# Two inner layer seams: the next layer's first chunk of matmuls taken one block of tokens at a time

## The reference

```python
# layers 0 and 1
h = rms_norm(x, pre_norm_w[i])
y = gated_deltanet_mixer(h, ...) if i == 0 else short_conv_mixer(h, ...)
x = x + rms_norm(y, post_norm_w[i])
# short_conv_mixer: u, b_gate, c_gate, z = split(h @ w_in, 4)
# layer 2
shift, scale, gate = split(c @ w_ada + b_ada, 3)
h = rmsnorm(x, pre_norm_g) * (1 + scale) + shift
proj = h @ w_in          # split in q, k, v, z_ret, u_val, u_gate, z_conv, g_a, g_b
```

## Time and profile before

| | |
|---|---|
| Median of 3 runs | 862.86 us (862.37 to 863.36) |
| Profiled execution: time, span of its rows | 862.82 us, 860.7 us |
| TensorE busy, DVE busy, ACT busy | 849.1 us (99%), 725.1 us (84%), 495.3 us (58%) |
| Mean granted TensorE clock | 0.999 |
| Seam 1, from the end of `gdn_out` to the second chunk of `sc_in` | 256.90 to 269.86 us |
| Seam 2, from the end of `sc_out` to the second chunk of `glu` | 487.20 to 501.31 us |

### The profile page before, as it was taken

How to read it: one execution, slowest core, us unless ns; L and a number is a source line. 1 busy time by engine, 2 the same in 40 slices (tenths; PEclk the granted TensorE clock), 3 DMA queues, 4 the chain that set the end, 5 groups by cost and what they waited for, 6 DMA issues and landing times.

```text
span 860.7 us, 14398 instructions
## 1 busy us (share of the span) xinstructions
PE 849.1 (99%) x5404; PEld 747.8 (87%) x5404; DVE 725.1 (84%) x1154; ACT 495.3 (58%) x726; POOL 47.7 (6%) x48
## 2 busy tenths in 40 slices
PE   9999999999999999999999999999999999999997
PEld 8999998798888888888888799999887798888885
DVE  7798999757858888989879788999998999957864
ACT  6878856566547555555546574433446674545743
POOL 0001001241100000000000000000001230001000
PEclk9999999999999999999999999999999999999999
DMA  8774684700783777777785554554454536564431
GB/s 270 248 255 133 195 277 147 191 3 4 276 292 94 239 252 255 254 255 252 250 306 196 195 172 150 194 193 165 166 181 137 176 107 199 193 231 159 163 131 49
DMA packets 129423, 163.63 MB, mean 190 GB/s; under 512 B 17203, under 2 KB 91867, under 8 KB 129243
## 3 DMA queue, kind: packets, MB, share of 16 engines
q1 hardware_dynamic: 129371, 162.92, 57.4%
HBM read 158.68 MB, written 4.23 MB: 189 GB/s over the span
## 4 chain that ended last, share of the span: by engine, by line
PE 85%; DVE 7%; DMA 3%; ACT 2%; issue 2%; SPq 0%; DVEq 0%; ACTq 0%
PE psum L583 12%; PE psum L570 12%; PE psum L584 11%; PE psum L590 11%; PE psum L551 7%; PE psum L558 7%; PE psum L552 7%; PE psum L575 6%; PE psum L843 3%; DMA w_raw<-in_sc_w_out_dram 2%; DVE w_lo L1543 1%; DVE Tq L1819 1%; DVE outer L1817 1%; PE psum L726 1%; PE psum L962 1%
## 5 line engine op out<-in xcount | busy, mean ns | idle before, releaser
L1040 ACT ACTIVATE w_hi<-w_raw 128x1024 fp32r<-128x1024 f32 x263 | 275.2, 1058 | 199.2 <-PE psum L590 98.2
L1543 DVE TENSOR_TENSOR w_lo<-w_raw,w_hi 128x1024 fp32r<-128x1024 f32 x264 | 316.3, 1223 | 69.6 <-ACT w_hi L1040 67.2
L551 PE MATMUL psum<-hT,w_hi 128*128 128x256 f32 x544 | 135.4, 287 | 0.0
L552 PE MATMUL psum<-hT,w_hi 128*128 128x256 f32 x544 | 133.4, 283 | 0.0
L570 PE MATMUL psum<-hT,w_hi 128*128 128x512 f32 x496 | 124.2, 392 | 0.0
L583 PE MATMUL psum<-w_hi,hT 128*128 128x512 f32 x288 | 116.6, 405 | 0.0
L584 PE MATMUL psum<-w_hi,hT 128*128 128x512 f32 x288 | 112.4, 390 | 0.0
L2062 DVE SCALAR_TENSOR_TENSOR cv<-aP,par,cv 128x256 f32<-128x256 f32 x240 | 106.9, 514 | 0.0
L551 PEld LDWEIGHTS psum<-hT,w_hi 128*128 128x128 f32 x544 | 104.3, 192 | 0.5 <-issue 0.2
L552 PEld LDWEIGHTS psum<-hT,w_hi 128*128 128x128 f32 x544 | 104.3, 192 | 0.4 <-issue 0.2
L570 PEld LDWEIGHTS psum<-hT,w_hi 128*128 128x128 f32 x496 | 89.2, 189 | 15.9
(11 more groups left out here) (313 smaller groups left out, 1059.5 us busy)
## 6 DMA issues: line engine op xcount, KB each, us to landing
w_raw<-in_w_in_dram SPq DMA_DIRECT2D x44, 1024.0 KB, 5.0
w_raw<-in_sc_w_in_dram SPq DMA_DIRECT2D x32, 1024.0 KB, 7.4
w_raw<-in_gdn_w_in_dram SPq DMA_DIRECT2D x23, 1024.0 KB, 6.9
ada<-in_w_ada_dram SPq DMA_DIRECT2D x24, 512.0 KB, 4.8
w_raw<-in_gdn_w_out_dram SPq DMA_DIRECT2D x8, 1024.0 KB, 5.2
w_raw<-in_sc_w_out_dram SPq DMA_DIRECT2D x8, 1024.0 KB, 7.5
w_raw<-in_w_ret_out_dram SPq DMA_DIRECT2D x8, 1024.0 KB, 5.1
w_raw<-in_w_conv_out_dram SPq DMA_DIRECT2D x4, 1024.0 KB, 5.1
```

The source lines that it names most:

```text
L551: pe.matmul(o[:, m, :], w_hi[s][:, k, mine], a_hi[:, ka, :], start=m == 0 and ka == 0, stop=False, skip_group_check=True)
L552: pe.matmul(o[:, m, :], w_hi[s][:, k, mine], a_lo[:, ka, :], start=False, stop=False, skip_group_check=True)
L1040: act.activation(w_hi[j % 2 * 2 + h][:, :, :], raw[slot][:, h * KH2:(h + 1) * KH2, :], ACT.Copy).then_inc(hi_ready, 1)
L1543: return dve.tensor_tensor(o, whole, hi.bitcast(F32), ALU.subtract)
```

## The change

In both inner seams the work is cut by blocks of 128 tokens.

- DVE's `y_norm` now makes `xn` of block 0 before `x_next` of block 1. What is left of block 1's norm moves to a new `block_norms` on ACT and DVE, which takes the place of `pre_norm` for `n` of 1 and 2. On ACT: four evictions of block 0, the squares and the root of block 1, four evictions of block 0, eight of block 1 (in seam 2 also two `hx` per block), a copy of block 0's sums, the split of the next chunk's first half, a copy of block 1's sums. Each eviction is 128x128.
- TensorE's `first_tokens` takes the place of `pre_norm` and `first_chunk`: it turns block 0 and computes, with the activations stationary and the weights moving, the first chunk for these 128 tokens in halves, with the turning of block 1 in the middle. The fillers are one and three, after the turning of block 0.
- The sums of the first chunk now lie as tokens by channels. ACT copies them to `tok`, and `turn_back` turns them with four transposes inside the next chunk, behind its first matmuls on `w_hi` (`midway`). The other chunks are as before.
- The first sums of `sc_in` have no separate part any more: ACT drops one `sc_part` copy, DVE's `sc_whole` becomes a `tensor_copy`, and the loops of ACT and DVE have their first step written out (`apart`).
- `fold_modulation` moves from behind `sc_out` to between the two token blocks of its last chunk.
- The `held` bounds in `chunks` are written differently; with the values used (0 and 1) they give the same order. The outer seam (`n == 0`) is only renamed.

```diff
+            def turn_block(n, t):
+
+                for k in range(KT):
+                    if k % KH2 == 0:
+                        pe.wait_ge(xn_ready, (NT * n + t) * 2 + k // KH2 + 1)
+                    mm = pe.transpose(block_of(t, k), xn[:, t, k * P:(k + 1) * P], ident)
+                    if k % KH2 == KH2 - 1:
+                        mm.then_inc(turned, 1)
+
+            def first_tokens(n, g, fill):
+
+                def high(t, h):
                     s = g % 2 * 2 + h
-                    if g == 0 and h == 0:
-                        pe.wait_ge(quarter_hi, 1)
-                    else:
-                        pe.wait_ge(hi_ready, 2 * g + h + 1)
+                    pe.wait_ge(hi_ready, 2 * g + h + 1)
                     for k in range(h * KH2, (h + 1) * KH2):
-                        if g == 0 and k == 2:
-                            pe.wait_ge(hi_ready, 1)
-                        pe.wait_ge(hhi_ready, KT * n + k + 1)
-                        for m in range(2):
-                            mine = slice(m * P, (m + 1) * P)
-                            pe.matmul(o_hi[:, m, :], w_hi[s][:, k % KH2, mine], hT_hi[:, k, :], start=k == 0 and (m == 0 or apart), stop=False,
-                                      skip_group_check=True)
+                        pe.wait_ge(hhi_ready, highs_by(n, t, k))
+                        pe.matmul(sums_of(t), hT_hi[:, k, tokens(t)], w_hi[s][:, k % KH2, :], start=k == 0, stop=False, skip_group_check=True)
                     pe.wait_ge(lo_ready, 2 * g + h + 1)
                     for k in range(h * KH2, (h + 1) * KH2):
-                        for m in range(2):
-                            mine = slice(m * P, (m + 1) * P)
-                            pe.matmul(o_hi[:, m, :], w_lo[s][:, k % KH2, mine], hT_hi[:, k, :], start=False, stop=False, skip_group_check=True)
+                        pe.matmul(sums_of(t), hT_hi[:, k, tokens(t)], w_lo[s][:, k % KH2, :], start=False, stop=False, skip_group_check=True)
+
+                def low(t, h):
+                    s = g % 2 * 2 + h
                     for k in range(h * KH2, (h + 1) * KH2):
                         if k % 2 == 0:
-                            pe.wait_ge(h_ready, KT // 2 * n + k // 2 + 1)
-                        for m in range(2):
-                            mine = slice(m * P, (m + 1) * P)
-                            mm = pe.matmul(o_lo[:, m, :], w_hi[s][:, k % KH2, mine], hT_lo[:, k, :], start=False, stop=k == KT - 1, skip_group_check=True)
-                    mm.then_inc(half_done, 1)
-
-            def chunk(i, g0, j, a_hi, a_lo):
+                            pe.wait_ge(h_ready, lows_by(n, t, k))
+                        mm = pe.matmul(sums_of(t), hT_lo[:, k, tokens(t)], w_hi[s][:, k % KH2, :], start=False, stop=k == KT - 1, skip_group_check=True)
+                    return mm
+
+                turn_block(n, 0)
+                keep_clock(fill[0])
+                high(0, 0)
+                keep_clock(fill[1])
+                low(0, 0)
+                high(0, 1)
+                turn_block(n, 1)
+                low(0, 1).then_inc(block_done, 1)
+                high(1, 0)
+                high(1, 1)
+                low(1, 0).then_inc(half_done, 1)
+                low(1, 1).then_inc(block_done, 1)
+
+            def turn_back(n, o):
+
+                for t in range(NT):
+                    pe.wait_ge(tok_copied, NT * (n - 1) + t + 1)
+                    for m in range(2):
+                        mm = pe.transpose(o[:, m, tokens(t)], tok[:, t, m * P:(m + 1) * P], ident)
+                mm.then_inc(half_done, 1)
+
+            def chunk(i, g0, j, a_hi, a_lo, midway=None):
 
                 o = bank(j)
                 pe.wait_ge(bank_free, i * 4 + (g0 + j + 1))
@@ -550,6 +616,8 @@
                             ka = h * KH2 + k
                             pe.matmul(o[:, m, :], w_hi[s][:, k, mine], a_hi[:, ka, :], start=m == 0 and ka == 0, stop=False, skip_group_check=True)
                             pe.matmul(o[:, m, :], w_hi[s][:, k, mine], a_lo[:, ka, :], start=False, stop=False, skip_group_check=True)
+                    if midway is not None and h == 0:
+                        midway()
                     pe.wait_ge(lo_ready, i * 8 + (2 * (g0 + j) + h + 1))
                     for m in range(2):
                         mine = slice(m * P, (m + 1) * P)
@@ -558,7 +626,7 @@
                             mm = pe.matmul(o[:, m, :], w_lo[s][:, k, mine], a_hi[:, ka, :], start=False, stop=ka == KT - 1, skip_group_check=True)
                     mm.then_inc(half_done, 1)
 
...
+                        elif ahead and j == 0 and midway is not None:
+                            continue
...
             wide_deep("gdn_out", yT_hi, yT_lo, (y_op_ready, 0), start=(ROUNDS - OUT_FROM) // 2)
 
             pe.wait_ge(bank_free, 4 + FIRST["gdn_out"] + 4)
-            pre_norm(1, (5, 0))
-            keep_clock(1)
-            phase("sc_in", hT_hi, hT_lo, first=(1, psum[:, 0:2, 0:SEQ], psum[:, 0:2, SEQ:2 * SEQ], True))
-            wide_deep("sc_out", yT_hi, yT_lo, (y_op_ready, KT))
-
-
-            pe.wait_ge(ada_used, MOD_PARTS)
-            pe.wait_ge(bank_free, 4 + FIRST["sc_out"] + 4)
-            for q in range(P // BS):
-                mm = pe.matmul(psum[q * BS:(q + 1) * BS, 0, 0:3 * KT], fold[:, :], mod_p[:, :, q], start=True, stop=True)
-            mm.then_inc(mod_done, 1)
-            pre_norm(2, (4, 0))
-            keep_clock(1)
+            first_tokens(1, FIRST["sc_in"], (1, 3))
+            pe.wait_ge(tok_copied, 1)
+            phase("sc_in", hT_hi, hT_lo, midway=lambda: turn_back(1, psum[:, 0:2, 0:SEQ]))
+
+            def fold_modulation():
+                pe.wait_ge(ada_used, MOD_PARTS)
+                pe.wait_ge(bank_free, 4 + FIRST["sc_out"] + 4)
+                for q in range(P // BS):
+                    mm = pe.matmul(psum[q * BS:(q + 1) * BS, 0, 0:3 * KT], fold[:, :], mod_p[:, :, q], start=True, stop=True)
+                mm.then_inc(mod_done, 1)
+            wide_deep("sc_out", yT_hi, yT_lo, (y_op_ready, KT), between=fold_modulation)
+            first_tokens(2, FIRST["glu"], (1, 3))
```

On ScalarE:

```diff
+            def block_norms(n, g, gain, shift=None):
+
+                def highs(t, ks):
+                    for k in ks:
+                        act.wait_ge(turned, turned_by(n, t, k))
+                        if shift is None:
+                            act.activation(hT_hi[:, k, tokens(t)], block_of(t, k), ACT.Copy, scale=gain(k)).then_inc(hhi_ready, 1)
+                        else:
+                            act.activation(hT_hi[:, k, tokens(t)], block_of(t, k), ACT.Identity, scale=gain(k), bias=shift(k)).then_inc(hhi_ready, 1)
+                    if shift is not None and ks[-1] == KT - 1:
+                        for k in (KT - 2, KT - 1):
+                            act.activation(hx[:, k, tokens(t)], block_of(t, k), ACT.Identity, scale=gain(k), bias=shift(k)).then_inc(hhi_ready, 1)
+
+                def copied(t):
+                    act.wait_ge(block_done, 3 * (n - 1) + 2 + t)
+                    act.activation(tok[:, t, :], sums_of(t), ACT.Copy).then_inc(tok_copied, 1)
+
+                if shift is not None:
+                    act.wait_ge(mod_ready, 1)
+                    act.wait_ge(gain2_ready, 1)
+                highs(0, range(KH2))
+                for q in range(2):
+                    x_square(n, 1, q)
+                x_root(n, 1)
+                highs(0, range(KH2, KT))
+                highs(1, range(KT))
+                copied(0)
+                split_hi(g, 0, 1, 0)
+                copied(1)
...
                             x_square(n + 1, 0, 1)
                             x_root(n + 1, 0)
-                            for q in range(2):
-                                x_square(n + 1, 1, q)
-                            x_root(n + 1, 1)
```

On VectorE:

```diff
+            def block_norms(n, g, gain, shift=None):
+
+                def lows(t, h):
+                    ks = range(h * KH2, (h + 1) * KH2)
+                    if shift is None:
+                        dve.wait_ge(hhi_ready, highs_by(n, t, ks[-1]))
+                        for k in ks:
+                            i = dve.scalar_tensor_tensor(out=hT_lo[:, k, tokens(t)], in0=block_of(t, k), scalar=gain(k),
+                                                         in1=hT_hi[:, k, tokens(t)].bitcast(F32), op0=ALU.mult, op1=ALU.subtract)
+                            if k % 2:
+                                i.then_inc(h_ready, 1)
+                        return
+                    dve.wait_ge(hhi_ready, highs_by(n, t, ks[-1]) + 2 * h)
+                    for k in ks[:KH2 - 2 * h]:
+                        i = dve.tensor_scalar(hx[:, k, tokens(t)], block_of(t, k), gain(k), shift(k), ALU.mult, ALU.add)
                     i.then_inc(hx_ready, 1)
-
-                for kp in range(KT // 2):
-                    dve.wait_ge(hhi_ready, KT * n + 2 * kp + 2)
-                    if shift is not None:
```

(77 more changed lines are left out.)

197 lines of the change are left out of this document (109 added, 88 removed).

## The result

The changed kernel takes 871.42 us in the median of 4 runs (869.84 to 871.79), the one before, beside it, 863.0 (862.37 to 863.36): a ratio of 1.0094 [1.0082, 1.0106], slower by 8.4 us. The profiled execution took 871.4, its span 869.3.

What follows compares the result with a forecast made beforehand. TensorE was taken as the bound, busy 849.1 of 860.7 us and waiting at the seams. TensorE's own order cost +1.85 us; with waits and `turn_back`, +2.1 and +2.65 made +4.75, so 867.6 us, range 865.2 to 871.8.

Steps and rivals of the forecast that it cites:

- seam 2: The gap on TensorE from the end of `sc_out` to the second chunk of `glu`; forecast +2.1 us, +2.65 with `turn_back`.
- the likeliest case: Whole kernel: both seams get longer at full clock, +4.75 us in sum, 867.6 us (866 to 870.4), chance 0.63.
- the clock falls: Rival: TensorE's rest before block 0's transposes halves its clock, some 2 us per seam; 869.6 to 873, chance 0.17.
- the five and four fillers ahead of the transposes: `keep_clock` calls on TensorE before block 0's transposes in the two inner seams; dropping them was put at nothing.
- seam 1: The gap on TensorE from the end of `gdn_out` to the second chunk of `sc_in`; forecast +1.55 us, +2.1 with `turn_back`.
- transposes sooner, from the end of `gdn_out`: Seam before `sc_in`: block 0's `xn` no longer waits behind block 1's `x` update, so its transposes start 1.09 us sooner.
- ACT's 128x128 evictions apart, seam 1 and 2: Spacing of ACT's narrow evictions from PSUM: 0.23 us before `sc_in`, 0.33 with bias before `glu`.
- wait on `w_lo` ahead of the second chunk: Before `sc_in`'s second chunk, TensorE waits about 1 us for DVE's split, which stands behind block 1's work.
- the fold ahead of `sc_out`'s last half chunk: The modulation's fold, 0.28 us, moved forward; costs nothing because ACT still squares `x` when that half chunk ends.
- `turn_back`, `sc_in` and `glu`: Four transposes on TensorE in the middle of the second chunk of each phase, 0.54 us each.
- Not slower: Rival: block 1's norm and evictions pass beneath block 0's matmuls, fillers fall into existing waits, splits are in time; 859.6, chance 0.07.
- both conditions named: Fillers and waits together under 0.9 us a seam; against it stood block 1's `xn`, 2 us later than before.

## Why the prediction was right or wrong

The 871.42 lies inside the range (865.2 to 871.8), and "slower" held, but the likeliest case, 867.6, was not what happened. The rival *the clock falls* was, in both seams, at 871.6; it had a chance of 0.17. That its sum came so close is partly luck: it took 4.0 us for the clock, of which the medians show 3.3, and 4.75 for all the rest, of which they show 5.3.

**The step that failed** is "the five and four fillers ahead of the transposes go too, but they ran in a wait and are worth nothing". They take no time from TensorE, but their work kept its clock: without them the kernel before loses 3.4 us (866.26 against 862.82; 1.8 in the seams of its profiled execution), with them the changed kernel gains 3.3. The rows named in the rival carried the right answer, a rest of 3 us against 0.90 and 1.15 before. I had set it at "some 2 us in each" seam; it was 1.6 and 0.7 in the profiled executions. In seam 2 it costs less since TensorE waits there for DVE anyway: block 1's `xn` came 5.70 us after the first transpose (501.38, 495.68), and 5.26 with the clock held, so 0.44 of the seam's 0.66 passed down that chain.

The Trainium skill ("TensorE: Matmul & The Clock Gate", Parts 1 and 4) was cited for this rival. The trace agrees with Part 1, that idleness sends the array to half rate. It does not show that transposes were part of the reason, as Part 4 has it: in seam 2 the clock was 0.83 in 495.00:495.50, before the first transpose at 495.68. Nor does it rule it out: in seam 1 the clock fell only at 263.0 to 263.5, behind the transposes and in a filler, and in seam 2 of the kernel before without its leading fillers some 1.1 us after the first transpose, at 493.84:

```profile
494.50:495.00 0.50, 0.46 (x5) 0.23 (x3) 0.50 (x2) 0.00 (x0) 0.00 (x0) 0.95 0.00 0
```

**The other steps** can be read in the kernel with the leading fillers, which is the case that the forecast worked out:

| step | forecast | measured |
|---|---|---|
| transposes sooner, from the end of `gdn_out` | 1.09 | 1.05 (261.40 - 257.13 against 261.65 - 258.43) |
| ACT's 128x128 evictions apart, seam 1 and 2 | 0.23, 0.33 | 0.25, 0.34 |
| seam 1 | +1.55 | +1.84 |
| wait on `w_lo` ahead of the second chunk | 1 | 0.76 |
| the fold ahead of `sc_out`'s last half chunk | 0 | 0.42 |
| seam 2 | +2.1 | +2.17 |
| `turn_back`, `sc_in` and `glu` | 0.54 each | 0.52, 0.42 |
| sum | +4.75 | +5.37, and +5.3 in the medians |

The forecast put the fold at nothing, since ACT would still be squaring `x` when the last half chunk ends. TensorE ends `sc_out` 0.42 later by it, and only the 0.28 that it took inside seam 2 comes back there.

The prices come from the timelines of ACT and DVE of the changed kernel:

```profile
262.52 1.14 ACT L1185 ACTIVATE hT<-psum,gain 128x128 fp32r<-128x128 f32 x4 [1.53 <-PE psum L561]
263.53 0.64 ACT L1149 ACTIVATE junk<-x 128x512 f32<-128x512 f32 x1
...
264.90 0.29 ACT L1154 ACTIVATE ms<-ss,part 128x1 f32<-128x1 f32 x1
...
496.91 1.50 ACT L1187 ACTIVATE hT<-psum,mod,gain 128x128 fp32r<-128x128 f32 x4 [2.01 <-PE psum L561]
```

```profile
261.22 0.88 DVE L1688 TENSOR_SCALAR xn<-x,rstd 128x512 f32<-128x512 f32 x2
...
265.59 0.88 DVE L1688 TENSOR_SCALAR xn<-x,rstd 128x512 f32<-128x512 f32 x2
...
273.38 1.22 DVE L1634 TENSOR_TENSOR w_lo<-w_raw,w_hi 128x1024 fp32r<-128x1024 f32 x1
```

Block 1's `xn` starts at 265.59, less the 1.44 of the late start 264.15, forecast 264.0 to 264.2; and DVE's split at 273.38 is what the second chunk waits for.

**Not slower** failed on both conditions named. Fillers and late split cost 1.7 in seam 1 where under 0.9 was needed, and block 1's norm comes too late: 7.02 us after the end of `gdn_out` (265.59 - 258.57) against 4.86 before (261.99 less 257.13). With the leading fillers, the old order of the norm, one inner filler (in seam 2) and the splits each in its place, the loss is 0.9 us instead of 8.4.

**Left open.** Seams, `turn_back` and the fold account for 7.65 of the 8.4 us (3.45 + 0.53 + 0.42 + 2.83 + 0.42). In the profiled executions the rest of the 8.6 is the 1.44 ahead of the change, less some 0.5 by which the kernel before waited longer in `sc_out`. Over the 12 profiled kernels the end of `gdn_out` lies between 257.13 and 258.98, and the kernel before without its leading fillers, which differs from it in nothing up to there, has 258.73. So I take it for scatter ahead of the change, but the medians are of 4 runs and no run was made to separate it.

## What to carry to other kernels

A filler in a wait has a price when it is taken away: before dropping it or moving it, find how long the engine then rests and what it does next. Cutting work in two so that the first half starts sooner only pays if the second half is not made later by it; follow the second half's chain first. And the best place for a prefetch step such as a split can differ from one seam to the next: the same move gained 0.9 us in one and lost 1.1 in the other.

## What the runs showed of the hardware

The clock fell after rests of 2.77, 3.13, 3.94 and 4.21 us at the head of a seam (in two of the four only 1 us or more after TensorE had begun to work again), and also in the middle of a seam, after 2.00 and 2.63 us of waiting. Each time TensorE then worked at 0.50 for some 3 us although it was busy nearly all that time (2.50 of 2.50, 2.83 and 3.00 of 3.00), and returned to 1.00. It stayed at 1.00 over rests of 0.90 to 1.28 us. ACT's and DVE's operations on 128 columns start 0.25 to 0.34 apart, well over half of the 0.36 to 0.46 for 256, so halving their tiles makes them dearer per element.
